# A two-layer hybrid decoder trunk on one Trainium2 core: the weight loads of the gated FFN's groups in the order in which their buffers come free, and the residual turned later

## The chip, the cores and the metric

The kernel runs on 1 core of one Trainium2 chip, in one launch. The metric is device time in microseconds (us), the median of several executions. Engines are named as in the profile: PE (TensorE), DVE (VectorE), ACT (ScalarE), POOL (GpSimd), SP (SyncE, which here only issues DMAs). SPq is SP's queue of DMA issues.

## The reference, cut to what matters

`x` is 512 tokens by 1024 channels, f32. There are two layers; each adds a mixer and then a gated FFN, and the change touches only the FFNs and the product that ends the second one.

```python
for l in range(2):
    h = rms_norm(x, mix_norm_w[l])
    y = even_mixer(h, ...) if l % 2 == 0 else odd_mixer(h, ...)
    x = x + y @ w_out[l]
    h = rms_norm(x, ffn_norm_w[l])                    # 512 x 1024
    x = x + (silu(h @ w_gate[l]) * (h @ w_up[l])) @ w_down[l]   # 1024 -> 2816 -> 1024
return rms_norm(x, final_norm_w)
```

## The kernel before

**Split products.** Every f32 product is made from operands that are split into a high and a low part (`hi` on ACT, `lo` on DVE) and multiplied as high*high + high*low + low*high. Weights come in tiles of 128x1024 f32 (512 KB). A tile's two parts live in one of the RING = 4 slots of `wring`; ACT may write a slot only when PE has used the tile four before it.

**The gated FFN.** `h @ w_gate` and `h @ w_up` share their left operand, and the kernel computes most of both (GROUPED = 5 groups of 512 columns each; 256 columns are done plainly before them) by a scheme with 7 block products for 8. A group `j` of layer `l` has GLU_PRODUCTS = 7 products of two tiles (p0, p1), so 14 steps: G_M11 (steps 0, 1), G_M12 (2, 3), G_M22 (4, 5), G_M21 (6, 7), G_SUM (8, 9), G_LAST (10, 11), G_ALL (12, 13). Their weights come from four buffers of two tiles each:

- `x_part` holds G_M11's tiles, then is added to in place three times for G_M21, G_SUM and G_ALL;
- `raw` holds G_M12's tiles; `y_part` holds G_M22's and is then added to `x_part` by DVE (`sum_weights`, after steps 6 and 8);
- `w_part` is loaded and grown once for G_LAST.

SP issues the plain loads (`load_group`, `load_part`). POOL issues the growing ones: a DMA with `accum_op=add` that adds a part of the weights to a buffer in SBUF (`grow_group`, L907): two on `x_part` for G_M21 after G_M11's `lo`, two on `w_part`, and two on `x_part` for G_ALL after G_SUM's `lo`. A next group's buffer may be loaded when the last `lo` that reads it is done: `raw` after G_M12, `y_part` after the sums of steps 6 and 8, `w_part` after G_LAST, `x_part` after G_ALL, the last two steps.

PE begins a group's G_M11 when DVE has taken G_LAST's result of the group before out of its PSUM bank (`gate_first`, L1600), which stands on DVE behind the `lo` of G_M11's p1 (step 1). It begins G_M12 after `up_second` (L1603), behind the `lo` of G_M12's p1 (step 3), and G_M21 after `q` (L1589, step 7).

**The residual.** The last product makes its result by tokens, while x is kept by channels, so x is turned: DVE transposes 32x32 blocks of xT into `turned` (`turn_residual`, L1630, eight instructions), and 16 DMAs on SP's queue (`residual_blocks`, L817, 128 KB each in pieces of 32 floats) put the blocks in their places in `resid`. `turned` lies over chunks of AF that ACT writes from group 2 on, and ACT waits for all 16 there (`keep_turned`, at step 7 of group 2 in layer 1).

**Order of the work.** All five engines run instruction lists written out by hand with semaphores; each engine and each DMA queue takes its list in order, so a DMA whose wait isn't over holds all that stand behind it.

**The last product** (`w_down` of layer 1) follows the same scheme on 42 tiles: `left_high` on ACT and `left_low` on DVE split its left operand's pieces (`place_even`, `place_odd`), and `halves` on DVE makes the sums that later products need.

A growth of one weight sum in DRAM (`w_sums`, 12 DMAs of POOL in the first mixer) is the same before and after.

Of the kernel before, what the change touches and what calls it, by code (L numbers as in the profile page):

```python
# [23 lines left out]
KD = D // P  # L24
# [12 lines left out]
GROUPED = 5  # L37
# [33 lines left out]
P_12, P_11, P_21, P_22, P_SUM, P_LAST, P_ALL = range(PRODUCTS)  # L71
# [9 lines left out]
def piece_rows(i):  # L81

    return range(2 * i, min(2 * i + 2, HALF))
# [18 lines left out]
def glu_tile(l, j, a, p):  # L102

    return T_GLU[l] + j * GLU_STEPS + 2 * a + p
# [7 lines left out]
def weights_summed(l, j, p):  # L112

    return l * SUMS + LEFT_SUMS + 2 * j + p + 1


def part_count(l, j):

    return 16 * (1 + GROUPED * l + j + 1)
# [22 lines left out]
def last_tile(g):  # L142

    return T_DN1 + g
# [222 lines left out]
def build(nc, sums_d, x_d, w_d, glu_d, last_d, vec_d, row_d, const_d, rope_d, final_d, out_d):  # L367
# [9 lines left out]
    def at(name, shape, dt, offset):  # L377
        t = nc.alloc_sbuf_tensor_at(name, [P] + list(shape), dt, offset=offset)
        return t, offset + (int(np.prod(shape)) * size[dt] + 31) // 32 * 32

    base = 16512
    xT, p = at("xT", [KD, S], f32, base)
    raw, p = at("raw", [RAW, TILE], f32, p)
    wring, p = at("wring", [RING, 2, TILE], f32r, p)
    at_H = p
    HH, p = at("HH", [KD, 2, S], f32r, p)
    consts, p = at("consts", [6 + len(LEVELS), P], f32, p)
    at_work = p
    hbuf, p = at("hbuf", [2, S], f32, p)
    sqb, p = at("sqb", [2, S], f32, p)  # L390
    squares, _ = at("squares", [4, S], f32, at_work)
    ssq, p = at("ssq", [S], f32, p)
    rstd, p = at("rstd", [S], f32, p)
    vec, p = at("vec", [N_VEC], f32, p)
# [117 lines left out]
    x_part, q = at("x_part", [2, TILE], f32, q)  # L512
# [5 lines left out]
    turned, _ = at("turned", [NB, KD, P], f32, at_A + 6 * S * 4)  # L518
# [14 lines left out]
    resid, _ = at("resid", [NB, 2, S], f32, base)  # L533
# [57 lines left out]
    def kept_chunk(k):  # L591

        return AF[:, k] if k < ENDING else kept_end[:, k - ENDING]
# [32 lines left out]
    def sem(name):  # L626
        if name not in sems:
            sems[name] = nc.alloc_semaphore(name)
        return sems[name]

    def slot_round(t):

        return t // RING + 1
# [9 lines left out]
    def raw_before(t):  # L643

        return max(u for u in range(t) if (uses_raw(u) or u < FIRST) and u % RAW == t % RAW and (t >= FIRST + RAW or u == t - FIRST))
# [13 lines left out]
    feed_hi, feed_sq, ssq_done, h_ready = map(sem, ("feed_hi", "feed_sq", "ssq_done", "h_ready"))  # L659
# [43 lines left out]
    FINAL = 4  # L703
# [16 lines left out]
    def _(sp):  # L720
# [41 lines left out]
        def load_part(l, place, sem_at, j, kh, u):  # L762

            for p in range(2):
                n = sem_at + p
                if j:
                    t = glu_tile(l, j - 1, G_LAST if place is w_part else G_M22 if place is y_part else G_ALL, p)
                    sp.wait_ge(lo_ready[t % RING], slot_round(t))
                    if place is y_part:
                        sp.wait_ge(sem("lhs_made"), weights_summed(l, j - 1, p))  # L770
                sp.wait_ge(part_loaded[n], part_count(l, j) - 16)
                sp.dma_start(place[:, p], glu_d[l, j, kh, u][:, p * TILE:(p + 1) * TILE]).then_inc(part_loaded[n], 16)

        def load_group(l, j):

            if j == 0:
                load_part(l, x_part, 0, j, 0, 0)
            for p in range(2):
                t = glu_tile(l, j, G_M12, p)
                before = raw_before(t)  # L780
                sp.wait_ge(hi_ready[before % RING], slot_round(before))
                sp.wait_ge(lo_ready[before % RING], slot_round(before))
                sp.dma_start(raw[:, t % RAW], glu_d[l, j, 0, 1][:, p * TILE:(p + 1) * TILE]).then_inc(raw_loaded[t % RAW], 16)
            load_part(l, y_part, 2, j, 1, 1)
            load_part(l, w_part, 4, j, 1, 0)
            if j + 1 < GROUPED:
                load_part(l, x_part, 0, j + 1, 0, 0)

        sp.wait_ge(tile_used, T_OUT0 + RING)
        for j in range(GROUPED):  # L790
            load_group(0, j)
# [12 lines left out]
                src = w_d[bass.ds(r * RING + (j - AWAY), 1)].rearrange("a p c -> (a p) c")  # L804
                sp.dma_start(raw[:, j % RAW], src).then_inc(raw_loaded[j % RAW], 16)

        def residual_blocks(m):

            a, b = m // 4, m % 4
            if m == 0:  # L810
                sp.wait_ge(sem("resid_turned"), KD)
                sp.wait_ge(feed_sq, KD * FINAL)
                sp.wait_ge(h_ready, KD * FINAL)
                sp.wait_ge(sem("lhs_scaled"), 2 * KD)
            to = resid[32 * b:32 * b + 32].rearrange("p t u (n x c) -> p (t u n) x c", x=4, c=32)
            from_ = turned[32 * a:32 * a + 32].rearrange("p t n (x c) -> p (t n) x c", c=32)
            sp.dma_start(to[:, :, a], from_[:, :, b]).then_inc(sem("resid_loaded"), 16)  # L817

        for t in range(loop_end * RING, T_GLU[1]):
            sp.wait_ge(hi_ready[(t - RAW) % RING], slot_round(t - RAW))  # L820
            sp.wait_ge(lo_ready[(t - RAW) % RING], slot_round(t - RAW))
# [1 line left out]
        sp.wait_ge(tile_used, T_GU1)  # L823
        for j in range(GROUPED):
            load_group(1, j)
            if j == 0:
                for m in range(16):
                    residual_blocks(m)

        for i in range(PIECES):  # L830
            t = last_tile(i)
# [3 lines left out]
            n = len(piece_rows(i)) * S  # L835
# [12 lines left out]
        for i in range(PIECES):  # L848
            t = last_tile(P_21 * PIECES + i)
# [7 lines left out]
        n = OUT_ORDER[-1]  # L857
# [622 lines left out]
    def _(dve):  # L1480
# [132 lines left out]
        def halves(r):  # L1613

            if r == 0:
                dve.wait_ge(sem("ffn_mul"), MULS + 2)
            else:
                dve.wait_ge(sem("glu_kept"), 4 * GROUPED + (2 * r if r < HALF - 2 else 4 * GROUPED - HALF + 1 + r))
            first, second = kept_chunk(2 * r), kept_chunk(2 * r + 1)
            V.tensor_tensor(first[:, 2 * P:S], first[:, 2 * P:S], second[:, 2 * P:S], ALU.subtract).then_inc(sem("halves_made"), 1)  # L1620
            dve.wait_ge(sem("halves_made"), 2 * r + 1)
            V.tensor_tensor(pfull[:, r], first[:, 0:2 * P], first[:, 2 * P:S], ALU.subtract).then_inc(sem("halves_made"), 1)
# [9 lines left out]
        def after_glu_lo(l, g):  # L1632

            j, step = divmod(g, GLU_STEPS)
            if j:
                if step == 1:
                    glu_results(l, j - 1, "gate_first")
                elif step == 3:
                    glu_results(l, j - 1, "up_second")
                    glu_results(l, j - 1, "first")  # L1640
                elif step == 4:
                    glu_results(l, j - 1, "second")
            elif l and 4 <= step < 8:
                for n in (2 * step - 8, 2 * step - 7):
                    turn_residual(n)
            if step == 6:
                sum_weights(l, j, 0)
            elif step == 7:
                glu_results(l, j, "q")
            elif step == 8:  # L1650
                sum_weights(l, j, 1)
            elif step == 9:
                glu_results(l, j, "up_first")
            elif step == 11:
                glu_results(l, j, "gate_second")
            if l and step in (10, 12):
                if j:
                    halves(2 * j - 1 + (step - 10) // 2)
                elif step == 10:
                    halves(0)  # L1660
# [6 lines left out]
        def left_low(a, i):  # L1667

            dve.wait_ge(sem("ffn_hi"), split_count(a, i))
            high = place(a, i, 0).bitcast(f32)  # L1670
            if a in (P_21, P_22):
                ins = V.scalar_tensor_tensor(place(a, i, 1), full_left(a, i), -1.0, high, ALU.mult, ALU.subtract)
            else:
                ins = V.tensor_tensor(place(a, i, 1), full_left(a, i), high, ALU.subtract)  # L1674
            ins.then_inc(sem("ffn_lo"), 1)
# [94 lines left out]
        def last_product():  # L1770

            dve.wait_ge(sem("resid_loaded"), 16 * 16)
            for g in range(PRODUCTS * PIECES):
                last_lo(g)
                a, i = divmod(g, PIECES)
                if g < RING:
                    group_end(1, g)
                if g == 4:
                    halves(9)
                    halves(10)  # L1780
                    left_low(P_12, 4)
                    left_low(P_12, 5)
                if a == P_22:
                    cross(P_LAST, i)
                if g < 36:
                    left_low(a + 1, i)
                if a == P_SUM:
                    cross(P_ALL, i)
                if i == 4 and a >= 2:
                    after_product(a - 1)  # L1790
# [34 lines left out]
        for n in range(KD):  # L1825
            dve.wait_ge(x_loaded[X_PART[n]], 16)
            feed_lo(0, n)
            if n < 2 * HALVED:
                t, half = n // 2, slice(n % 2 * S, (n % 2 + 1) * S)
# [53 lines left out]
        for kind, a in even_order():  # L1883
# [26 lines left out]
            elif kind == "gate_evac":  # L1910
                c, m = SLOTS[a][1:]
# [18 lines left out]
            elif kind == "tap":  # L1930
                c, k = a
# [1072 lines left out]
```

## Time and profile before

| | before |
|---|---|
| median of 3 runs | 1222.06 us (1219.14 to 1222.58) |
| profiled execution, its own time | 1221.2 us |
| its span, first to last instruction | 1219.4 us |
| PE matmul busy | 1186.4 us, 97% of the span |
| DVE, ACT, POOL busy | 837.8, 619.4, 141.9 us |
| mean granted clock of PE | 0.990 |
| chain that ended last, PE's share | 85%; SPq 2%, nearly all on L817 |

Matmul ends are modelled, so a busy PE is not PE at its peak; but PE's idle time is what waits for other engines cost here. A time such as 926 us is counted from the span's start. The first FFN's groups run from about 245 to 446 us, the second's from 886 to 1105 us, the last product from there to 1203 us.

### The profile page before, as it was taken

How to read it: one execution, taken by the hardware profiler on the slowest of the kernel's cores; microseconds unless marked ns; L12 is line 12 of the kernel's file. 1: busy time of each engine (PE TensorE's matmuls, PEld its weight loads, DVE VectorE, ACT ScalarE, POOL GpSimd, SP SyncE). 2: the span in 40 equal slices, each digit the busy share in tenths (PEclk: the TensorE clock that was granted, in tenths of full speed). 3: DMA queues.
4: the chain of work that ended last, by engine and by line, in shares of the span. 5: the costliest groups of instructions: out<-in, count | busy, mean ns of one | idle time of the engine just before them, and what ended most of it. 6: DMA issues, size and time to landing. Idle time of an engine off the chain costs nothing.

```text
span 1219.4 us, 15948 instructions
## 1 busy us (share of the span) xinstructions
PE 1186.4 (97%) x5791; PEld 959.2 (79%) x5791; DVE 837.8 (69%) x1273; ACT 619.4 (51%) x992; POOL 141.9 (12%) x251
## 2 busy tenths in 40 slices
PE   9999999999999999999999999999995899999998
PEld 7876648888888888888888788888874788887886
DVE  6787886786667763336777666546791777788796
ACT  6354455655555543235584254444551555556564
POOL 0010000011111100000003814300010111110120
PEclk9999999999999999999999999999998899999999
DMA  6388621567877843222322211012558587777981
GB/s 246 121 230 184 153 54 52 192 102 209 206 155 159 247 97 104 95 96 74 110 78 68 87 36 53 27 60 70 181 96 187 124 210 204 171 175 271 226 151 69
DMA packets 63694, 165.45 MB, mean 136 GB/s; under 512 B 22658, under 2 KB 22914, under 8 KB 63362
## 3 DMA queue, kind: packets, MB, share of 16 engines
q1 hardware_dynamic: 49746, 114.33, 28.9%
q0 software_dynamic: 12960, 48.76, 22.4%
q10 hardware_dynamic: 912, 1.35, 0.4%
q8 instruction: 47, 0.77, 0.3%
q14 instruction: 29, 0.24, 0.1%
HBM read 155.87 MB, written 10.75 MB: 137 GB/s over the span
## 4 chain that ended last, share of the span: by engine, by line
PE 85%; DVE 6%; ACT 3%; SPq 2%; issue 2%; DMA 2%; ACTq 0%; DVEq 0%
PE PS L2263 82%; SPq L817 2%; PE PS L2559 1%; DMA first_raw<-w_stream 1%; DVE wring L1571 1%; PE PS L2339 1%; DVE cacc L1939 0%; DMA x_part<-w_glu 0%; ACTq L1275 0%; DVE wring L1794 0%; DMA raw<-w_glu 0%; ACT wring L1036 0%; ACT wring L984 0%; DVE turned L1630 0%; DVE amax L1857 0%
## 5 line engine op out<-in xcount | busy, mean ns | idle before, releaser
L2263 PE MATMUL PS<-HH,wring 128*128 128x512 f32 x1176 | 288.7, 397 | 0.9 <-DVE vd L2191 0.9
L2263 PE MATMUL PS<-wring,HH 128*128 128x512 f32 x1152 | 268.7, 392 | 17.6 <-DVE glu_s L1603 17.3
L2263 PEld LDWEIGHTS PS<-wring,HH 128*128 128x128 f32 x1152 | 217.2, 189 | 63.4 <-DVE glu_s L1603 17.7
L2263 PEld LDWEIGHTS PS<-HH,wring 128*128 128x128 f32 x1176 | 215.0, 188 | 44.0 <-issue 1.3
L1571 DVE TENSOR_TENSOR wring<-x_part,wring 128x1024 fp32r<-128x1024 f32 x80 | 97.9, 1224 | 77.3 <-ACT wring L1036 77.2
L1794 DVE TENSOR_TENSOR wring<-raw,wring 128x1024 fp32r<-128x1024 f32 x91 | 111.9, 1232 | 46.2 <-ACT wring L984 46.2
L984 ACT ACTIVATE wring<-raw 128x1024 fp32r<-128x1024 f32 x91 | 95.7, 1056 | 94.4 <-PE PS L2263 68.8
L1036 ACT ACTIVATE wring<-x_part 128x1024 fp32r<-128x1024 f32 x80 | 84.6, 1060 | 107.1 <-PE PS L2263 45.9
L2263 PE MATMUL PS<-AS,wring 128*128 128x512 f32 x528 | 120.4, 389 | 0.0
L2263 PE MATMUL PS<-wring,left_minus 128*128 128x512 f32 x480 | 113.8, 393 | 1.6 <-DVE glu_q L1589 1.6
L2263 PEld LDWEIGHTS PS<-AS,wring 128*128 128x128 f32 x528 | 99.0, 188 | 20.5
L2263 PEld LDWEIGHTS PS<-wring,left_minus 128*128 128x128 f32 x480 | 88.9, 188 | 19.9 <-DVE glu_q L1589 2.0
L907 POOL DMA_DIRECT2D x_part<-w_glu x40 | 34.6, 865 | 454.4 <-DVE wring L1571 454.4
L2263 PE MATMUL PS<-AA,wring 128*128 128x512 f32 x264 | 63.4, 394 | 0.4 <-DVE AA L1873 0.3
L2263 PE MATMUL PS<-wring,place_even 128*128 128x512 f32 x264 | 61.1, 390 | 1.2 <-DVE place_even L1674 1.2
L2263 PEld LDWEIGHTS PS<-wring,place_even 128*128 128x128 f32 x264 | 49.4, 188 | 11.8 <-issue 1.6
L2263 PEld LDWEIGHTS PS<-AA,wring 128*128 128x128 f32 x264 | 49.1, 188 | 11.6 <-issue 1.0
L2263 PE MATMUL PS<-wring,left_diff 128*128 128x512 f32 x240 | 56.5, 391 | 0.4 <-DVE hbuf L1600 0.4
L2263 PEld LDWEIGHTS PS<-wring,left_diff 128*128 128x128 f32 x240 | 44.8, 188 | 10.7 <-DVE hbuf L1600 1.5
L1665 DVE TENSOR_TENSOR AS<-AF,AS 128x512 fp32r<-128x512 f32 x20 | 13.8, 689 | 48.0 <-ACT AS L1087 48.0
L2263 PE MATMUL PS<-wring,place_odd 128*128 128x512 f32 x198 | 45.4, 389 | 0.0
L2263 PEld LDWEIGHTS PS<-wring,place_odd 128*128 128x128 f32 x198 | 37.2, 188 | 7.7
(367 smaller groups left out, 1687.8 us busy)
## 6 DMA issues: line engine op xcount, KB each, us to landing
raw<-w_stream SPq DMA_DIRECT2D x91, 512.0 KB, 3.5
x_part<-w_glu POOLq DMA_DIRECT2D x40, 512.0 KB, 6.3
x_part<-w_glu SPq DMA_DIRECT2D x20, 512.0 KB, 4.3
raw<-w_glu SPq DMA_DIRECT2D x20, 512.0 KB, 5.8
y_part<-w_glu SPq DMA_DIRECT2D x20, 512.0 KB, 8.6
w_part<-w_glu SPq DMA_DIRECT2D x20, 512.0 KB, 13.9
w_part<-w_glu POOLq DMA_DIRECT2D x20, 512.0 KB, 7.1
w_sums<-w_last POOLq DMA_DIRECT2D x12, 704.0 KB, 6.7
```

What stands on the lines that cost most here:

```text
L817: sp.dma_start(to[:, :, a], from_[:, :, b]).then_inc(sem("resid_loaded"), 16)
L907: nc.gpsimd.dma_start(to, addend[:, p * TILE:(p + 1) * TILE], accum_op=ALU.add).then_inc(added[d % ADDING], 16)
L984: nc.scalar.activation(wring[:, t % RING, 0], raw_tile(t), ACT.Copy).then_inc(hi_ready[t % RING], 1)
L1036: nc.scalar.activation(wring[:, t % RING, 0], glu_source(t, a, p), ACT.Copy).then_inc(hi_ready[t % RING], 1)
L1571: V.tensor_tensor(wring[:, t % RING, 1], glu_source(t, a, p), wring[:, t % RING, 0].bitcast(f32), ALU.subtract).then_inc(lo_ready[t % RING ...
L1665: V.tensor_tensor(AS[:, k % RING, 1], kept_chunk(k), AS[:, k % RING, 0].bitcast(f32), ALU.subtract).then_inc(sem("ffn_lo"), 1)
L1794: V.tensor_tensor(wring[:, t % RING, 1], raw_tile(t), wring[:, t % RING, 0].bitcast(f32), ALU.subtract).then_inc(lo_ready[t % RING], 1)
L2263: return nc.tensor.matmul(out, lhsT, rhs, start=start, stop=stop, skip_group_check=adds)
L2339: last = nc.tensor.transpose(PS[:, bank, blk(j)], src[:, u % 2, blk(j)], ident)
L2559: last = nc.tensor.transpose(PS[:, banks[c], blk(b)], glu_result(b)[:, blk(c)], ident)
```

## The change

Three edits, all of them in the order of instructions; no operation is added or removed.

1. **Loads.** In both layers SP's list for group `j` was: raw(j), y(j), w(j), x(j+1). It becomes raw(j), y(j), w(j), x(j), so that of a next group's eight loads `x_part`'s two, whose buffer comes free last, stand last and not first.
2. **Residual.** The 16 DMAs stood behind x(1) and ahead of raw(1). Now 8 stand between raw(2) and y(2), and 8 between y(2) and w(2). DVE's eight transposes move from steps 4 to 7 of group 0 to steps 10, 12 and 13.
3. **Last product.** At its tile 4 DVE splits pieces 4 and 5 of the first left operand before it makes `halves(9)` and `halves(10)`, no longer after.

```diff
@@ SP
-            if j == 0:
-                load_part(l, x_part, 0, j, 0, 0)
+        def load_group(l, j):
+
+            if j == 0:
+                load_part(l, x_part, 0, j, 0, 0)
+            load_raw(l, j)
+            if l and j == 2:
+                for m in range(8):
+                    residual_blocks(m)
             load_part(l, y_part, 2, j, 1, 1)
+            if l and j == 2:
+                for m in range(8, 16):
+                    residual_blocks(m)
             load_part(l, w_part, 4, j, 1, 0)
-            if j + 1 < GROUPED:
-                load_part(l, x_part, 0, j + 1, 0, 0)
+            if j:
+                load_part(l, x_part, 0, j, 0, 0)
...
             load_group(1, j)
-            if j == 0:
-                for m in range(16):
-                    residual_blocks(m)
@@ DVE, after_glu_lo
-            elif l and 4 <= step < 8:
-                for n in (2 * step - 8, 2 * step - 7):
+            elif l and step in (10, 12, 13):
+                for n in {10: (0, 1), 12: (2, 3, 4), 13: (5, 6, 7)}[step]:
                     turn_residual(n)
@@ DVE, last_product
                 if g == 4:
+                    left_low(P_12, 4)
+                    left_low(P_12, 5)
                     halves(9)
                     halves(10)
-                    left_low(P_12, 4)
-                    left_low(P_12, 5)
```

(`load_raw` holds the two loads of `raw` as they stood in `load_group`, now L793.)

SP's list in layer 1, from the end of group 0's loads to x(2), before the change:

```order
L772 DMA w_part<-w_glu 128x1024 [waits x_loaded5]
L772 DMA x_part<-w_glu 128x1024 [waits x_loaded0,lo_ready1]
L772 DMA x_part<-w_glu 128x1024 [waits x_loaded1,lo_ready2]
L817 DMA resid<-turned 32x32x32 [waits h_ready,lhs_scaled,feed_sq,resid_turned]
L817 DMA resid<-turned 32x32x32 x15
L783 DMA raw<-w_glu 128x1024 [waits lo_ready3,hi_ready3]
L783 DMA raw<-w_glu 128x1024 [waits lo_ready0,hi_ready0]
L772 DMA y_part<-w_glu 128x1024 [waits x_loaded2,lhs_made,lo_ready1]
L772 DMA y_part<-w_glu 128x1024 [waits x_loaded3,lhs_made,lo_ready2]
L772 DMA w_part<-w_glu 128x1024 [waits x_loaded4,lo_ready3]
L772 DMA w_part<-w_glu 128x1024 [waits x_loaded5,lo_ready0]
```

and group 2's loads in the list of the changed kernel, which SP issues while group 1 runs:

```order
L793 DMA raw<-w_glu 128x1024 [waits lo_ready1,hi_ready1]
L793 DMA raw<-w_glu 128x1024 [waits lo_ready2,hi_ready2]
L784 DMA resid<-turned 32x32x32 [waits h_ready,lhs_scaled,feed_sq,resid_turned]
L784 DMA resid<-turned 32x32x32 x7
L772 DMA y_part<-w_glu 128x1024 [waits x_loaded2,lhs_made,lo_ready3]
L772 DMA y_part<-w_glu 128x1024 [waits x_loaded3,lhs_made,lo_ready0]
L784 DMA resid<-turned 32x32x32 x8
L772 DMA w_part<-w_glu 128x1024 [waits x_loaded4,lo_ready1]
L772 DMA w_part<-w_glu 128x1024 [waits x_loaded5,lo_ready2]
L772 DMA x_part<-w_glu 128x1024 [waits x_loaded0,lo_ready3]
L772 DMA x_part<-w_glu 128x1024 [waits x_loaded1,lo_ready0]
```

Each load now stands behind loads whose waits end earlier than its own, and the 16 small DMAs stand ahead of y(2), w(2) and x(2).

DVE's list in group 0 of layer 1, before (from step 4 to the first growth's `q`):

```order
L1630 STREAM_TRANSPOSE turned<-xT 128x4x128 x2
L1571 TENSOR_TENSOR wring<-y_part,wring 128x1024
L1630 STREAM_TRANSPOSE turned<-xT 128x4x128 x2
L1571 TENSOR_TENSOR wring<-x_part,wring 128x1024
L1630 STREAM_TRANSPOSE turned<-xT 128x4x128 x2
L1578 TENSOR_TENSOR x_part<-x_part,y_part 128x1024
L1571 TENSOR_TENSOR wring<-x_part,wring 128x1024
L1630 STREAM_TRANSPOSE turned<-xT 128x4x128 x2
L1589 TENSOR_TENSOR glu_q<-PS,glu_q 128x512 x2
```

and in the changed kernel, from step 10 on:

```order
L1637 STREAM_TRANSPOSE turned<-xT 128x4x128 x2
L1627 TENSOR_TENSOR AF<-AF 128x256
L1629 TENSOR_TENSOR pfull<-AF 128x256
L1578 TENSOR_TENSOR wring<-w_part,wring 128x1024
L1602 TENSOR_TENSOR glu_q<-glu_q,PS 128x512 x2
L1578 TENSOR_TENSOR wring<-x_part,wring 128x1024
L1637 STREAM_TRANSPOSE turned<-xT 128x4x128 x3
L1578 TENSOR_TENSOR wring<-x_part,wring 128x1024
L1637 STREAM_TRANSPOSE turned<-xT 128x4x128 x3
L1578 TENSOR_TENSOR wring<-x_part,wring 128x1024 x2
L1607 TENSOR_TENSOR hbuf<-PS,glu_s 128x512 x2
```

The transposes have left the stretch ahead of `q` (L1589) and stand round the two `lo` of G_ALL.

## Rows read from the trace of the kernel before

**Rows 1.** Waits of PE, longest first (four of fifteen)

```profile
PE PS L2263 <- DVE glu_s L1603: 17.3, 1, 17.3
PE PS L2263 <- DVE glu_q L1589: 1.6, 1, 1.6
...
PE PS L2263 <- DVE place_even L1674: 1.2, 1, 1.2
...
PE PS L2263 <- DVE hbuf L1600: 0.4, 1, 0.4
```

**Rows 2.** Timeline of SP: start, duration, what (xcount)

```profile
918.16 20.49 SPq L817 DMA_DIRECT2D resid<-turned  x16
938.74 1.11 SPq L783 DMA_DIRECT2D raw<-w_glu  x2
```

**Rows 3.** Chain that ended last, 914 to 965 us: start, us, what

```profile
919.81 2.43 SPq L817
...
932.82 0.67 SPq L817
...
949.18 7.77 PE PS L2263 x24
...
957.82 5.49 PE PS L2263 x24
```

**Rows 4.** One stretch of 1 us: busy time by engine, clock, DMA share, GB/s

```profile
936.00:937.00 1.00, 0.00 (x0) 0.00 (x0) 0.00 (x0) 0.00 (x0) 0.00 (x0) 0.75 1.09 180
```

**Rows 5.** Timeline of DVE, group 0 of layer 1 (one of four pairs)

```profile
893.40 1.30 DVE L1630 STREAM_TRANSPOSE turned<-xT 128x512 f32<-128x512 f32 x2
```

**Rows 6.** Timeline of DVE, last product, tile 4

```profile
1117.14 0.43 DVE L1620 TENSOR_TENSOR AF<-AF 128x256 f32<-128x256 f32 x1 [2.85 <-ACT AF L1043]
...
1118.73 0.68 DVE L1674 TENSOR_TENSOR place_even<-AF,place_even 128x512 fp32r<-128x512 f32 x1
```

**Rows 7.** Chain that ended last, from group 1 to 2 of layer 0

```profile
317.05 5.21 DMA x_part<-w_glu
```

**Rows 8.** Timeline of PE: first matmuls of groups 2 and 3, layer 1

```profile
985.80 1.52 PE L2263 MATMUL PS<-wring,left_diff 128*128 128x512 f32 x6
...
1025.70 5.60 PE L2263 MATMUL PS<-wring,left_diff 128*128 128x512 f32 x24
```

**Rows 9.** Timeline of ACT there: `hi` of G_ALL p1, of the next G_M11 p1

```profile
1015.08 1.06 ACT L1036 ACTIVATE wring<-x_part 128x1024 fp32r<-128x1024 f32 x1 [0.43 <-PE PS L2263]
...
1021.32 1.06 ACT L1036 ACTIVATE wring<-x_part 128x1024 fp32r<-128x1024 f32 x1 [1.69 <-DMA x_part<-w_glu]
```

**Rows 10.** Timeline of DVE there: `lo` of G_LAST p0, G_ALL p1, then `gate_first`, `sum_weights` p1

```profile
1008.01 1.23 DVE L1571 TENSOR_TENSOR wring<-w_part,wring 128x1024 fp32r<-128x1024 f32 x1 [0.42 <-ACT wring L1036]
...
1016.17 1.22 DVE L1571 TENSOR_TENSOR wring<-x_part,wring 128x1024 fp32r<-128x1024 f32 x1 [0.69 <-ACT wring L1036]
...
1023.56 1.28 DVE L1600 TENSOR_TENSOR hbuf<-PS,glu_s 128x512 f32<-128x512 f32 x2
...
1042.72 1.22 DVE L1578 TENSOR_TENSOR x_part<-x_part,y_part 128x1024 f32<-128x1024 f32 x1
```

**Rows 11.** Timeline of POOL there: the growth of G_ALL p1

```profile
1006.69 0.87 POOL L907 DMA_DIRECT2D x_part<-w_glu  x1 [2.62 <-DVE wring L1571]
```

**Rows 12.** DMA issues of 1017:1017.7, 938:941: xcount, KB, us to landing

```profile
x_part<-w_glu SPq DMA_DIRECT2D x1, 512.0 KB, 3.9
...
y_part<-w_glu SPq DMA_DIRECT2D x2, 512.0 KB, 6.4
```

**Rows 13.** DMA issues of POOL at 1006.69, 984.80, 925.12 and 1136.83

```profile
x_part<-w_glu POOLq DMA_DIRECT2D x1, 512.0 KB, 6.2
...
x_part<-w_glu POOLq DMA_DIRECT2D x1, 512.0 KB, 12.1
...
x_part<-w_glu POOLq DMA_DIRECT2D x1, 512.0 KB, 7.8
...
kept<-w_last POOLq DMA_DIRECT2D x1, 256.0 KB, 9.1
```

More of the change, by code:

```diff
@@ L772, in load_part, with residual_blocks, load_raw @@
                 sp.dma_start(place[:, p], glu_d[l, j, kh, u][:, p * TILE:(p + 1) * TILE]).then_inc(part_loaded[n], 16)
-        def load_group(l, j):
-            if j == 0:
-                load_part(l, x_part, 0, j, 0, 0)
+        def residual_blocks(m):
+            a, b = m // 4, m % 4
+            if m == 0:
+                sp.wait_ge(sem("resid_turned"), KD)
+                sp.wait_ge(feed_sq, KD * FINAL)
+                sp.wait_ge(h_ready, KD * FINAL)
+                sp.wait_ge(sem("lhs_scaled"), 2 * KD)
+            to = resid[32 * b:32 * b + 32].rearrange("p t u (n x c) -> p (t u n) x c", x=4, c=32)
+            from_ = turned[32 * a:32 * a + 32].rearrange("p t n (x c) -> p (t n) x c", c=32)
+            sp.dma_start(to[:, :, a], from_[:, :, b]).then_inc(sem("resid_loaded"), 16)
+        def load_raw(l, j):
             for p in range(2):
@@ L805, in _ @@
                 sp.dma_start(raw[:, j % RAW], src).then_inc(raw_loaded[j % RAW], 16)
[L807 to L817, printed above, removed]
         for t in range(loop_end * RING, T_GLU[1]):
```

## The prediction

> **What bounds the kernel now.** I read the table of busy times first: PE's matmuls fill nearly all of the span, so a gain can only come from PE's idle time and from stretches at the low clock. So the second view is the list of PE's waits [rows 1]. One wait is 17.3 us long, and three more lie where the edits are: 1.6, 1.2 and 0.4 us; all others lie elsewhere.
>
> The timeline of SP tells what the long one is. After x(1) SP issues the residual's 16 small DMAs, which takes from 918.16 to 938.65, and only then raw(1) [rows 2]. PE is through G_M11(1) at 949.18 - 17.3 = 931.9 [rows 1, 3] and can't start G_M12(1): `up_second` stands on DVE behind the `lo` of raw(1), and PE goes on at 949.18 [rows 3]. SP is the bound in this stretch, and it is held by its queue. The issues are slow only for a part of the time: two by 919.81, then six up to 932.82, 2.2 us each, then eight in 5.8 us, 0.73 each [rows 2, 3]. The slow part ends when POOL's growth of 925.12 has landed, 7.8 us later at 932.9 [rows 13]. So small DMAs give way to a growth, and hardly slow it: alone it takes 6.2.
>
> The pause also costs clock. PE went idle at 931.9 and the granted clock fell within 936 to 937 to half [rows 4]; the first 24 matmuls after it took 7.77 us, against 5.49 for the next 24 [rows 3]: 2.3 us more.
>
> **What the groups look like where nothing stalls.** Let t be the time since PE began a group's G_M11. From group 2 to 3 of layer 1 the period is 39.9 us [rows 8]. The `hi` of G_ALL p1 begins at t = 29.3, held by PE [rows 9]; its `lo` ends at 31.6 [rows 10], x's p1 is issued, lands after 3.9 [rows 12] at 35.5, where ACT waited for it [rows 9]; `gate_first` ends at 39.0 [rows 10]. That is 3.5 us from landing to release, and PE needs it at 39.9: the margin is 0.9 us. The growth of x's p1 for G_ALL is issued at t = 20.9 [rows 11] and lands at 27.1; it may land at 29.3 without being noticed, and at 30.1 before PE waits. Every group boundary hangs on this chain.
>
> **The change, part by part.**
>
> *The long wait.* Raw(1)'s two loads now stand behind w(0) and x(0) and wait for G_M12(0) alone, with nothing of the residual ahead of them, so they land some 20 us before they are wanted. The 17.3 us go, and with them the 2.3 us of half clock: 19.6. What hides the loads is group 0 itself.
>
> *The transposes.* Four pairs of 1.30 us [rows 5] stood on DVE ahead of `q`, 5.2 us, and PE waited 1.6 for `q` [rows 1]. Without them `q` is in time: gain 1.6. At steps 12 and 13 three each take 1.95 us. Ahead of the `lo` of G_ALL p1 DVE has 0.7 us of idle time in a quiet group [rows 10]; 1.95 - 0.7 = 1.3 us late, less the margin of 0.9, is 0.4 in the worst order I can make. Bounds 0 and 1.3 (no margin); I take 0.3.
>
> *The last product.* Four instructions of `halves` fill DVE from 1117.14 to 1118.73, where the split of piece 4 begins [rows 6], for which PE waits 1.2 us [rows 1]. The new order gives these 1.6 us to the split first; the wait goes: gain 1.2. The halves are then late by about 1 us, the two splits; they feed products whose tiles aren't next.
>
> *Layer 0.* The 0.4 us wait [rows 1] stands where x's p1 took 5.21 us to land [rows 7], with raw, y and w issued right behind it. With nothing behind it I take 3.9: gain 0.4.
>
> Sum of the gains: 17.3 + 2.3 + 1.6 + 1.2 + 0.4 = 22.8 us.
>
> *The residual's new place.* The 16 DMAs still go through SP's queue, now in group 1. The first eight follow raw(2), at t of about 3; they delay only y(2), which isn't wanted for 40 us. The second eight follow y(2)'s p1, which waits for the second weight sum, done at t = 1043.94 - 1025.70 = 18.2 [rows 8, 10]. Behind them stand w(2), free at t = 23.4 [rows 10], and x(2), whose p1 is free at 31.6 and is on the chain above. Price: from 18.7 two quick issues to 20.3; then at 2.2 us each until the growth of t = 20.9 has landed, 7.8 later at 28.7: four; two more at 0.73: t = 30.2. Then w p0, w p1, x p0, x p1 in one burst. In the burst of 938.74 [rows 2] the third and fourth load took 6.4 us from issue [rows 12], the fourth being issued some 1.6 after the first: it lands 8.0 after the burst's start. So x p1 lands at 38.2, release at 41.7, a wait of 1.8 us. Bounds: nothing, if all eight go at 0.73 (t = 24.6, ahead of x); and 5.0, if they take the 14.7 us of the first eight before (t = 33.4), and 7.3 with the clock's 2.3, since the pause would then be about as long as the one after which the clock fell. The first eight meet w's growths, which now come early, and may make y's p1 late too; so I take 3.0, above the middle estimate.
>
> *Loads beside growths, in every group.* Before, a next group's raw, y and w were issued behind x, in a burst, when no growth was near its due time. Now y's p1 (t = 18.2), w's p0 (23.4) and p1 (about 26) travel while POOL grows x for G_ALL. How much this delays the growth that may land until 30.1 no row shows directly. From below: small DMAs beside it, 7.8 us [rows 13], lands at 28.7, no wait. From above: 12.1 us, beside six loads and another growth [rows 13]: lands at 33.0, a wait of 2.9 per boundary. The nearest row is a growth beside loads in the last product, 9.1 us [rows 13], though of half the size: 30.0, just in time. Seven boundaries (four per layer less the one above) at 0.3 us: 2.0.
>
> The sum of the losses is 0.3 + 3.0 + 2.0 = 5.3; the gain left is 17.5. Against the profiled execution's own time, 1221.2, this makes 1203.7. The median of the runs is 0.9 above that execution, so I predict 1204.5 us.
>
> The Trainium skill speaks against this part (*DMA: Bandwidth & Descriptors*, section *Queues, rings and completion order*): each DMA engine goes round robin between the queues that have work, a packet at a time. By it POOL's growths and SP's loads would halve the engines between them, whoever is urgent. The 12.1 us agree with that; the 7.8 us beside the small DMAs don't look like halves by time.
>
> **The rivals.**
>
> *Growths late everywhere.* If a growth shares evenly with each load that overlaps it, it pays for them: a load in a burst adds (8.0 - 3.9) / 3 = 1.4 us, so three moved loads add up to 4.2: the growth lands at up to 31.3, a wait of 1.2 at seven boundaries, 8.4; and the residual's place then costs its upper 5.0. Net gain 22.8 - 8.4 - 5.0 - 0.3 = 9.1: 1213. For it: the 12.1 us. Against: these loads come one by one, and the first of them is over before the critical growth begins to move data. By the Trainium skill's rule above this is the case that would come.
>
> *All hidden.* The eight go at 0.73 and no growth is late: 22.8 gained, 1199.3. For it: small DMAs hardly disturb growths, and 128 KB at 0.73 us is quick. Against: the slow issues before were slow just because two growths ran, and two run here.
>
> *Slower or no gain.* One mechanism at every boundary: the growth of G_ALL p1 lands not at 27 but past 33. From 12.1 us on, eight boundaries lose 2.9 each, 23.2, which is all that is gained; with the residual's 3.0 the kernel stands at 1225.5. It decides from a landing time of about 12.5 us. Against: it needs three loads spread over 8 us to do what six in a burst did.
>
> *The wait only moves.* SP's 20.5 us could reappear whole at group 1 to 2. They can't: the list is cut by y(2), which waits until 18.2, and raw(2) is ahead; what can move is the 5.0 to 7.3 above, 1207 to 1209, held in the range of the likeliest.
>
> **How the numbers follow.** The likeliest case, a chance of 0.55, has its own range from 1200.5 (the residual's place at 1, no growth late) to 1209 (7.3 there, or growths 0.9 late at each boundary). All hidden 0.15; growths late everywhere 0.24, 1210 to 1217; slower or no gain 0.06. Leaving out the tail below 1199 and what lies above 1215, less than 2 in 10, gives 1199 to 1215. A measurement of this kernel can tell about 0.3%, 3.7 us, from no change: 1218.4 and 1225.7 are the limits. The first three cases lie below the first: faster 0.94. The last is split: same 0.03, slower 0.03.
>
> **What the changed profile would show.** Right: PE's wait for `glu_s` gone and no stretch of half clock near 940; no wait for `glu_q` or `place_even`; SP's 16 small DMAs in two runs of eight, the second ending near t = 30 of group 1; one wait of 1 to 5 us for `hbuf` (`gate_first`) at the start of G_M11(2) in layer 1. Wrong: waits of 1 us and more for `hbuf` at most starts of groups, with POOL's growths of G_ALL taking 10 us and more to land; or the clock at half again in group 2; or, the other way, no wait there at all.

## The result, and the profile after

The changed kernel takes 1205.28 us, the median of 4 runs (1204.76 to 1206.66); the kernel before, beside it, 1221.98. The ratio is 0.987, with a 95% interval of 0.9852 to 0.9887. The profiled execution took 1204.76 us with a span of 1203.0, 16.4 less than before's 1219.4. The forecast was 1204.5.

The waits of PE after the change, the three longest of ten (engine, who released it: us in all, times, longest):

```profile
PE PS L2270 <- DVE hbuf L1607: 6.5, 2, 6.2
PE PS L2270 <- POOL rstd L872: 1.3, 1, 1.3
PE PS L2270 <- DVE vd L2198: 0.9, 1, 0.9
```

Against [rows 1]: the waits for `glu_s` (17.3), `glu_q` (1.6) and `place_even` (1.2) are gone, and so is layer 0's 0.4. One new wait of 6.2 us has come, for `hbuf` (`gate_first`). All lines are 7 further down than before: L1600 is now L1607.

The timeline of SP after, from the loads of group 1 to those of group 3 (start, duration, what), against [rows 2]:

```profile
911.27 3.24 SPq L772 DMA_DIRECT2D x_part<-w_glu  x2
923.47 2.18 SPq L793 DMA_DIRECT2D raw<-w_glu  x2
925.83 14.51 SPq L784 DMA_DIRECT2D resid<-turned  x8
940.44 3.03 SPq L772 DMA_DIRECT2D y_part<-w_glu  x2
943.53 12.71 SPq L784 DMA_DIRECT2D resid<-turned  x8
956.33 1.10 SPq L772 DMA_DIRECT2D w_part<-w_glu  x2
957.53 0.86 SPq L772 DMA_DIRECT2D x_part<-w_glu  x2
969.91 2.17 SPq L793 DMA_DIRECT2D raw<-w_glu  x2
```

Group 1 begins at 922.32. The second eight end at 956.24, t = 33.9, and x(2) goes out behind them and behind w(2). What that does is in the timelines of ACT and PE (the brackets hold the idle time ahead and what ended it):

```profile
953.30 1.06 ACT L1043 ACTIVATE wring<-x_part 128x1024 fp32r<-128x1024 f32 x1 [1.97 <-DMA x_part<-w_glu]
964.00 2.25 ACT L1043 ACTIVATE wring<-x_part 128x1024 fp32r<-128x1024 f32 x2 [8.66 <-DMA x_part<-w_glu]
```

```profile
922.32 5.78 PE L2270 MATMUL PS<-wring,left_diff 128*128 128x512 f32 x24 [0.28 <-DVE hbuf L1607]
968.76 7.62 PE L2270 MATMUL PS<-wring,left_diff 128*128 128x512 f32 x24 [6.21 <-DVE hbuf L1607]
976.22 5.61 PE L2270 MATMUL PS<-wring,HH 128*128 128x512 f32 x24
```

The first row of ACT is the `hi` of G_ALL p1: it waited 1.97 us for POOL's growth, which landed 9.9 us after its issue at 943.37 (the quiet group's took 6.2 [rows 13]). The second is the `hi` of the next G_M11, both tiles at once, at 964.00. PE stood still from 962.55 to 968.76, and its first 24 matmuls took 7.62 us against 5.61 for the next. So the new place of the residual cost 6.2 us of waiting and 2.0 of half clock.

The windows of 1 us there (PE busy, granted clock, DMA share, GB/s) show when the clock fell, as [rows 4] did:

```profile
964.00:965.00 1.00, 0.00 (x0) 1.00 0.22 86
965.00:966.00 1.00, 0.00 (x0) 0.99 0.00 0
966.00:967.00 1.00, 0.00 (x0) 0.50 0.02 8
```

PE had been idle for 3.4 us when the clock went from 2.4 to 1.2 GHz; it came back between 972 and 973, some 4 us after PE had begun again.

### The profile page after: what moved, and what is told of

The parts are those of the page before. It is cut to its first block, busy times and chain, and to the rows that moved or that the text cites. A ratio compares the mean times of both kernels' runs of the same rounds, so it can differ in the third digit from the quotient of the medians.

```text
span 1203.0 us, 15948 instructions
## 1 busy us (share of the span) xinstructions
PE 1184.6 (98%) x5791; PEld 958.4 (80%) x5791; DVE 837.4 (70%) x1273; ACT 619.1 (51%) x992; POOL 142.0 (12%) x251
## 4 chain that ended last, share of the span: by engine, by line
PE 88%; DVE 5%; ACT 3%; issue 2%; SPq 1%; DMA 1%; ACTq 0%; POOL 0%; DVEq 0%; POOLq 0%
PE PS L2270 85%; PE PS L2566 1%; SPq L784 1%; DMA x_part<-w_glu 1%; DVE wring L1578 1%; ACT wring L1043 1%; PE PS L2346 1%; DVE cacc L1946 0%; ACTq L1282 0%; PE PS L2650 0%; DVE wring L1801 0%; ACT wring L991 0%; DVE turned L1637 0%; DVE out L2261 0%; DVE hbuf L1607 0%
## 6 DMA issues: line engine op xcount, KB each, us to landing
w_part<-w_glu POOLq DMA_DIRECT2D x20, 512.0 KB, 11.2
```

## Experiments

Each was timed beside the kernel before in the same session (its medians there: 1219.8, 1220.6 and 1219.9 us), so runs are compared by their ratios.

### The second eight behind x(2)

```diff
-            if l and j == 2:
-                for m in range(8, 16):
-                    residual_blocks(m)
             load_part(l, w_part, 4, j, 1, 0)
             if j:
                 load_part(l, x_part, 0, j, 0, 0)
+            if l and j == 2:
+                for m in range(8, 16):
+                    residual_blocks(m)
```

> Two theories of the 6.2 us wait for `gate_first` at the start of G_M11(2) in layer 1 and the half clock behind it (2.0 us). *Order in SP's queue:* w(2) and x(2) were issued late because the second eight small DMAs stood ahead of them (12.7 us, to 956.2), and the growth for G_ALL(1) was late (9.9 us) because the eight ran beside it. With the eight behind x(2) they begin at about t = 32, beside the growths of group 2 as the first eight ran beside those of group 1 (about 14 us), and are through some 3 us before ACT waits for the residual at step 7 of group 2. Both 6.2 and 2.0 go: 1205.3 - 8.2 = 1197.1 us, a wait for `hbuf` there of at most 0.5 us, the clock full. *Growths beside the loads of y(2) and w(2):* the growth lands late (9 us and more) with or without the small DMAs; the wait shrinks to 2 to 4 us at the same place and the time is 1200 to 1203 us.

Measured: 1198.06 us, ratio 0.9824 (0.9809 to 0.984); the span is 1195.6, 7.4 less than the changed kernel's. Its timeline of SP, and the first matmuls of group 2:

```profile
946.28 3.05 SPq L772 DMA_DIRECT2D w_part<-w_glu  x2
951.73 3.04 SPq L772 DMA_DIRECT2D x_part<-w_glu  x2
954.82 19.78 SPq L784 DMA_DIRECT2D resid<-turned  x8
```

```profile
963.17 5.73 PE L2270 MATMUL PS<-wring,left_diff 128*128 128x512 f32 x24 [0.29 <-DVE hbuf L1607]
```

w(2) and x(2) go out at their buffers' own times, the wait is 0.3 us and the clock stays full: the order in SP's queue was the cause. The growth for G_ALL p1 still took 8.3 us beside y(2)'s loads, and that costs nothing. With the second eight beside it too it took 9.9 us in the changed kernel's first profile and 8.9 in its second. So against the 6.2 of a quiet group most of the delay goes with y(2)'s loads, and less of it with the second eight. The eight themselves took 19.8 us, more than the 14 expected: ACT waited 2.83 us for them at step 7 of group 2, PE not at all. This version beats both kernels. Once more, in another session:

> The version with the second eight behind x(2) once more, beside its neighbours: 0.982 of the kernel before, 1197 to 1199 us, no wait above 0.5 us for `hbuf`.

1197.74 us, ratio 0.9823 (0.981 to 0.9836), waits for `hbuf` 0.43 and 0.16 us, the growth for G_ALL p1 8.8 us.

### Four and four

```diff
-                for m in range(8, 16):
+                for m in range(8, 12):
                     residual_blocks(m)
             load_part(l, w_part, 4, j, 1, 0)
             if j:
                 load_part(l, x_part, 0, j, 0, 0)
+            if l and j == 2:
+                for m in range(12, 16):
+                    residual_blocks(m)
```

> Of the second eight small DMAs four stay behind y(2), four go behind x(2): the dose between the changed kernel and the one with all eight moved. *Order in SP's queue:* in the changed kernel the fourth of the eight is issued at 952.6, just as the growth lands, so the growth is about as late as there (9 to 10 us); but x(2) p1 is then held by the `lo` of G_ALL p1 alone (t = 33 instead of 34.2 and a burst of four loads): the wait for `hbuf` is 1.5 to 3 us and the clock stays full, 1198.5 to 1200 us. If only the count of DMAs ahead of x(2) mattered, in proportion: half of 6.2, 3.1 us, and 1201 us. *Growths beside the loads:* no different from the run with all eight moved.

Measured: 1201.42 us, ratio 0.9854 (0.9836 to 0.9871). SP and PE:

```profile
941.49 11.20 SPq L784 DMA_DIRECT2D resid<-turned  x4
952.79 1.11 SPq L772 DMA_DIRECT2D w_part<-w_glu  x2
953.99 1.15 SPq L772 DMA_DIRECT2D x_part<-w_glu  x2
```

```profile
966.24 5.74 PE L2273 MATMUL PS<-wring,left_diff 128*128 128x512 f32 x24 [3.38 <-DVE hbuf L1610]
```

Four DMAs hold SP for 11.2 us where eight held it for 12.7: most of the price of small DMAs in this place is one stretch of time, not a count, and each DMA issued behind it adds 0.7 us. The wait was 3.4 us, above the 1.5 to 3 that I gave, since SP came free only at 952.7 and w and x then went out in one burst. Wait and time lie nearer to what the count alone would give (3.1 us, 1201 us), so this run's time doesn't decide between the two; SP's rows do. The clock stayed full.

### All sixteen behind x(2)

```diff
-            if l and j == 2:
-                for m in range(8):
-                    residual_blocks(m)
             load_part(l, y_part, 2, j, 1, 1)
-            if l and j == 2:
-                for m in range(8, 16):
-                    residual_blocks(m)
             load_part(l, w_part, 4, j, 1, 0)
             if j:
                 load_part(l, x_part, 0, j, 0, 0)
+            if l and j == 2:
+                for m in range(16):
+                    residual_blocks(m)
```

> All sixteen of the residual's small DMAs behind x(2), none beside the growth for G_ALL(1). This also shows how long that growth takes beside the loads of y(2) and w(2) alone. *Order in SP's queue:* x(2) in time, no wait for `hbuf`, growth within 7.5 us; the sixteen take about 20 us from t = 32 and end some 3 us after ACT wants them at step 7 of group 2, and raw(3) goes out some 8 us later than before, still early: a wait of 0 to 2 us in group 2, 1197 to 1199 us. *Growths beside the loads:* the growth takes 9 us and more, and a wait of 1 to 3 us for `hbuf` stays: 1199 to 1202 us.

Measured: 1203.67 us, ratio 0.9872 (0.9856 to 0.9887), 5 us worse than expected. Rows of SP, ACT and PE:

```profile
954.36 26.77 SPq L784 DMA_DIRECT2D resid<-turned  x16
```

```profile
983.08 1.08 ACT L1047 ACTIVATE AF<-PS 128x512 f32<-128x512 f32 x2 [7.54 <-DMA resid<-turned]
```

```profile
963.20 5.74 PE L2267 MATMUL PS<-wring,left_diff 128*128 128x512 f32 x24 [0.90 <-DVE hbuf L1604]
983.82 0.41 PE L2563 MATMUL PS<-consts,hbuf 128*128 128x128 f32 x2 [3.08 <-ACT AF L1047]
984.64 7.32 PE L2267 MATMUL PS<-wring,left_minus 128*128 128x512 f32 x24
```

The sixteen took 26.8 us, not 20, and ended 7.5 us after ACT wanted them; PE waited 3.1, and the clock fell with it (7.32 against 5.7 for 24 matmuls). So the residual can also be too late: eight behind x(2) fit, sixteen don't. The growth for G_ALL p1, beside the loads of y(2) and w(2) alone and each at its own time, took 6.8 us, within the 7.5 expected, and the wait for `hbuf` was 0.9: the loads by themselves don't make it late.

### The growths for G_ALL(1) shrunk

```diff
-                nc.gpsimd.dma_start(to, addend[:, p * TILE:(p + 1) * TILE], accum_op=ALU.add)...
+                few = 16 if (l, j) == (1, 1) and n >= 4 else TILE
+                nc.gpsimd.dma_start(to[:, 0:few], addend[:, p * TILE:p * TILE + few], accum_op=ALU.add)...
```

> The changed kernel with POOL's two growths for G_ALL(1) in layer 1 cut to 16 of their 1024 columns (so most of the last weight sum of group 1 is left out); all waits and the order of SP's queue stay. *The growth makes the small DMAs slow:* the second eight go at about 0.73 us each, SP is through with them near 949.5 instead of 956.2, w(2) and x(2) p0 are issued at once, x(2) p1 as soon as its `lo` ends (t = 31.6); no wait for `hbuf`, full clock: 8.2 us less than the changed kernel, 1197 us. *They are slow by themselves, or beside y(2)'s two loads:* SP is through with them at 953 to 956 and 3 to 6 us of the wait stay: 1199 to 1205 us.

Measured: 1197.41 us, ratio 0.9818 (0.98 to 0.9836). SP, then PE:

```profile
941.07 9.77 SPq L784 DMA_DIRECT2D resid<-turned  x8
950.94 1.11 SPq L772 DMA_DIRECT2D w_part<-w_glu  x2
952.14 1.92 SPq L772 DMA_DIRECT2D x_part<-w_glu  x2
```

```profile
963.20 5.76 PE L2271 MATMUL PS<-wring,left_diff 128*128 128x512 f32 x24 [1.03 <-DVE hbuf L1608]
```

Neither theory came out whole. Without the growths' data the time is about that of the version with the second eight behind x(2), and the wait 1.0 us, but the eight still take 9.8 us and not the 5.8 of eight at 0.73: y(2)'s two loads, ahead of them in the same queue, hold them too. The trace bears this out: the third small DMA's issue stood from 943.05 to 947.17, y(2)'s second load landed at 947.4, and from 943 to 945 us the shrunk growths took 3.2% of the engines' time. No run had neither the loads nor the growths there.

### All sixteen ahead of y(2)

```diff
-                for m in range(8):
+                for m in range(16):
                     residual_blocks(m)
             load_part(l, y_part, 2, j, 1, 1)
-            if l and j == 2:
-                for m in range(8, 16):
-                    residual_blocks(m)
```

> All sixteen of the residual's DMAs between raw(2) and y(2): the second eight run beside the same growths for G_ALL(1) as in the changed kernel, but without y(2)'s two 512 KB loads ahead of them in SP's queue. With the growths shrunk and y(2)'s loads there they took 9.8 us; with both 12.4 to 14.3. *Both hold them, and add up:* 5.8 us when nothing does, 4.0 for y(2)'s loads, 2.6 to 4.5 for the growths; so here 8.4 to 10.3 us, through near t = 28. y(2), w(2) and x(2) p0 then go in one burst and x(2) p1 lands about 1.5 us late: 1198 to 1200 us. *The growths alone are enough:* 12 us and more, to t = 31, a wait of 4 us and more for `hbuf`: 1202 to 1205 us. *The loads in the queue alone:* 5.8 us, no wait, 1197 us.

Measured: 1203.45 us, ratio 0.9865 (0.9851 to 0.9879). SP and ACT:

```profile
926.66 26.94 SPq L784 DMA_DIRECT2D resid<-turned  x16
953.71 1.10 SPq L772 DMA_DIRECT2D y_part<-w_glu  x2
...
955.85 1.19 SPq L772 DMA_DIRECT2D x_part<-w_glu  x2
```

```profile
963.33 1.06 ACT L1040 ACTIVATE wring<-x_part 128x1024 fp32r<-128x1024 f32 x1 [8.72 <-DMA x_part<-w_glu]
```

The last eight took from 940.6 to 953.6, 13 us, though no load stood ahead of them: the growths alone are enough, and the two causes don't add. PE waited 4.8 us for `hbuf` and lost clock again; y(2), w(2) and x(2) all went out late, and a wait of 0.8 us came at the start of the next group too.

Why they are slow is in the DMA queues (packets, MB, time of the packets as a share of 16 engines; q0 is POOL's, q1 SP's), here 943 to 945 us of this run, in which SP's queue holds nothing but small DMAs:

```profile
q0 software_dynamic: 76, 0.31, 86.0%
q1 hardware_dynamic: 128, 0.02, 10.5%
```

and 954 to 957 us of the changed kernel, after the growth:

```profile
q1 hardware_dynamic: 4298, 0.54, 108.7%
```

A small DMA is some 1,024 packets of 128 bytes. Alone 4298 pass in 3 us, 0.71 us for a DMA, which is the 0.7 us of an issue. Beside a growth in full flow 128 pass in 2 us, fewer than two for each of its 76 large packets of about 4 KB; at that rate one DMA would take 16 us. It never comes to that, because the growths have thinner stretches: from 942 to 952 us, with both growths in it, 4949 small packets pass, 2.1 us for a DMA. The Trainium skill (*DMA: Bandwidth & Descriptors*, section *Queues, rings and completion order*) has each DMA engine go round robin between the queues that have work, a packet at a time. The rows agree in kind: turns are shared, time isn't, and the queue with the large packets gets 86% of it against 10.5%. The small ones are starved, and SP stands at its next issues meanwhile: three of the last eight took 2.0, 4.3 and 2.8 us.

### The loads' order alone, and the old order with the residual away

The loads alone: the changed kernel with the residual's 16 DMAs behind the loads of group 0, the transposes at steps 4 to 7 and the `halves` first.

```diff
             load_group(1, j)
+            if j == 0:
+                for m in range(16):
+                    residual_blocks(m)
```

> The new order of the loads alone: the residual's 16 DMAs stand behind the loads of group 0 and ahead of all of group 1's, the transposes are at steps 4 to 7, the `halves` ahead of the splits, all as in the kernel before. The residual can then start as soon as it is turned (t about 18), no longer behind x(1) at t = 32. *Order in SP's queue:* 16 DMAs take some 20.5 us, to t = 39; raw(1) lands in time, but x(1) p1 lands about 8 us later, at t = 47 instead of 35.5, so PE waits some 9 us for `hbuf` at the start of G_M11(1), plus 2 of half clock; with 1.6 for `q` and 1.2 for the last product back and no wait at G_M11(2): 1205.3 + 11.3 - 8.2 + 2.8 = 1211 us. So most of the 17.3 us wait goes by the load order alone and part of it moves. *Rival:* the residual's DMAs are quick there (0.73 each, 12 us in all, to t = 30): no wait at G_M11(1), 1200 us.

Measured: 1215.82 us, ratio 0.9966 (0.9953 to 0.9979). SP and ACT:

```profile
902.71 19.84 SPq L784 DMA_DIRECT2D resid<-turned  x16
```

```profile
934.89 1.06 ACT L1040 ACTIVATE wring<-x_part 128x1024 fp32r<-128x1024 f32 x1 [16.54 <-DMA x_part<-w_glu]
```

The sixteen took the 20 us I gave them, but x(1) stood last in a burst of eight loads and landed only at 934.9 and later: the wait for `hbuf` was 13.7 us, not 9. So the new order of loads alone turns the 17.3 us wait into one of 13.7; it pays only with the residual moved too.

The other half: the kernel before's order of loads, with the residual in group 2 behind w(2) and the two other edits as changed.

```diff
             load_part(l, w_part, 4, j, 1, 0)
+            if l and j == 2:
+                for m in range(16):
+                    residual_blocks(m)
             if j + 1 < GROUPED:
                 load_part(l, x_part, 0, j + 1, 0, 0)
```

> The kernel before with its own order of loads (x of the next group ahead of that group's raw, y and w), but the residual's sixteen DMAs in group 2 behind w(2), and the transposes and the `halves` as in the changed kernel. Asks what the load order is worth once the residual is out of the way. The long wait at G_M12(1) goes. The sixteen start near 957.5, behind x(2), raw(2), y(2) and w(2), and take 27 us as in the run with all of them behind x(2): ACT waits about 10 us for them at step 7 of group 2, of which PE sees 5 to 6, plus 2 us of half clock: 1203 to 1205 us. If the load order itself were worth something beside that (by the prediction 0.4 in layer 0), waits of 0.4 us and more would also come back at other starts of groups.

Measured: 1212.27 us, ratio 0.9931 (0.9917 to 0.9946), 8 us above what I expected. Of SP and PE:

```profile
959.71 30.48 SPq L784 DMA_DIRECT2D resid<-turned  x16
```

```profile
992.84 0.66 PE L2559 MATMUL PS<-consts,hbuf 128*128 128x128 f32 x2 [11.46 <-ACT AF L1043]
```

The sixteen, behind a burst of loads and beside four growths, took 30.5 us; ACT waited 15.0 and PE 11.5. In the old order x(2) is ahead of raw, y and w, so all of them go out late and the residual later still. It also shows in layer 0: this run has a wait of 1.2 us there at the start of a group, before has 0.4, and no profile in the new order has one. What the new order is worth beyond that this run doesn't settle, since it tries one place of the residual in the old order. Its own trace shows another: behind w(1) SP has nothing to issue from 921.1 to 952.98 us, when x(2)'s buffer comes free, 32 us in a row, and sixteen small DMAs in a row took 20 to 30 us wherever they stood. The old order with the residual there was not run; it is a rival to moving the loads at all.

### The transposes back, and the halves back

The changed kernel with each small edit undone, and the changed kernel itself as their comparison.

> The changed kernel unaltered, beside the next three, as what they are compared with. 1204 to 1206 us, with 6.2 us for `hbuf` at G_M11(2) and half clock behind it as in its first profile. The stretch near 783 us, which no edit touches, ran at half clock for some 4 us in the profile of before and of the loads alone and at full clock in the others: if it is chance of the run, single runs of one kernel lie about 1.6 us apart for it.

1204.70 us, ratio 0.9871 (0.9853 to 0.9889).

```diff
-            elif l and step in (10, 12, 13):
-                for n in {10: (0, 1), 12: (2, 3, 4), 13: (5, 6, 7)}[step]:
+            elif l and 4 <= step < 8:
+                for n in (2 * step - 8, 2 * step - 7):
```

> The changed kernel with the eight transposes back at steps 4 to 7 of group 0, all else as changed. If they cost what the prediction says: PE's wait of 1.6 us for `q` comes back, the wait of 0.3 us at the start of G_M11(1) goes: 1.3 us more than the changed kernel. *Rival:* the 1.6 us are swallowed by the margin behind (0.9 at most), or the 0.3 us is due to the growth beside the loads and stays: between 0.7 and 1.6 us more.

1206.63 us, ratio 0.9887 (0.9869 to 0.9906). The interval doesn't part it from the changed kernel, but its waits do:

```profile
PE PS L2270 <- DVE hbuf L1607: 5.9, 1, 5.9
PE PS L2270 <- DVE glu_q L1596: 1.6, 1, 1.6
```

The 1.6 us for `q` is back, and the wait at the start of G_M11(1) is gone: `hbuf` is waited for once. With the transposes at steps 12 and 13 that wait was 0.28 and 0.75 us in the changed kernel's two profiles, and 0 to 0.61 in the others that have them there. So the move gives 1.6 and takes back at most 0.75. From the start of group 0 to that of group 1 it is 40.0 us with the transposes back, and 38.5 and 39.0 in the changed kernel's two profiles: a net 1.0 to 1.5. That the transposes cause the wait at G_M11(1) isn't shown, since two of the profiles that have them there have no wait.

```diff
+                    halves(9)
+                    halves(10)
                     left_low(P_12, 4)
                     left_low(P_12, 5)
-                    halves(9)
-                    halves(10)
```

> The changed kernel with the `halves` ahead of the splits again in the last product. PE's wait of 1.2 us for `place_even` comes back and the time is 1.2 us longer; if another engine was as late there, PE's wait would be shorter and the time within 0.5 us of the changed kernel.

1205.30 us, ratio 0.9875 (0.9857 to 0.9893), which by itself tells nothing of 1.2 us. The waits do:

```profile
PE PS L2270 <- DVE hbuf L1607: 6.1, 2, 5.7
...
PE PS L2270 <- DVE place_even L1681: 1.2, 1, 1.2
```

and the span, 1204.2, is 1.5 longer than the 1202.7 of the changed kernel's second profile, whose waits for `hbuf` add up to 6.2.

## Why the prediction was right, and where it was wrong

The likeliest case came, inside its own range, with its sign, place and mechanism. But one of the signs that the prediction lists as *wrong* came too: the clock was at half again at the start of group 2, behind a wait of 6.2 us where 1 to 5 were given. The 16.4 us of span come apart by the starts of the groups as follows.

| from the start of | before, us | after, us | gained, us |
|---|---|---|---|
| the kernel to group 0 of layer 1 | 885.95 | 883.80 | 2.15: layer 0 0.5, the stretch at 783 us 1.6 |
| group 0 to group 1 | 40.13 | 38.52 | 1.6 |
| group 1 to group 2 | 59.72 | 46.44 | 13.3 |
| group 2 to group 3 | 39.90 | 41.92 | -2.0: half clock |
| group 3 to the last product | 79.80 | 79.88 | -0.1 |
| the last product to the end | 113.9 | 112.4 | 1.5 |

*The long wait*: 19.6, as predicted. From the start of group 1 to that of group 2 in layer 1 it was 59.72 us before and is 46.44, of which 6.21 are the new wait; 59.72 - 19.6 = 40.1 and 46.44 - 6.21 = 40.2 are the same period. *The transposes*: the 1.6 for `q`, as predicted, and the undoing shows it. The 0.3 lost at the start of group 1 is there in this profile, but it is 0 to 0.75 in the others, so the 0.3 predicted is neither shown nor refuted; the net of group 0 is 1.6. *The last product*: the 1.2 of waiting went and came back with the edit; the part is 1.5 shorter, and 0.3 of that no wait explains. *Layer 0*: 0.5 instead of 0.4, by the start of its group 3 (405.79 before, 405.26 after).

*Loads beside growths*: I charged 2.0 us, 0.3 at each of seven boundaries. The periods of the quiet groups are 39.9 to 40.1 us after as before, so it cost 0.3 us at most. The growth for G_ALL p1 is indeed later, 6.4 us for group 2's against 6.2 [rows 13] and 8.3 beside y(2)'s loads without small DMAs behind them, but it lands when PE's own pace releases its `hi`. The rival *growths late everywhere* fell with that: the one growth that is late enough to be waited for is the one with y(2)'s loads in full and the second eight beside it.

*The residual's new place*: this step failed in its size. I took 3.0 us, with 7.3 as the upper bound; it cost 8.2, 6.2 of waiting and 2.0 of clock. The eight ended at t = 33.9, not 30.2, and x(2) p1 landed in time for 964.0, t = 41.7, not 38.2. The chain that ended last has the two slow issues:

```profile
944.17 5.45 SPq L784
...
949.66 2.91 SPq L784
```

I had the slow stretch end at t = 28.7, since I let the growth land after 7.8 us; it took 9.9 (8.9 in the second profile), and the stretch ended at 30.3: 1.5 us. And I priced the slow issues at 2.2 us each, an average of [rows 3], so that only two would be left at the end of the stretch; with only these two issued in it, five were left at 0.7: 2.2 us more. A third number I put at nothing: y(2)'s two loads, which are ahead of the eight in SP's queue. From 944 to 949 us of the changed kernel, most of the first slow issue, the two queues moved

```profile
q1 hardware_dynamic: 257, 0.95, 63.4%
q0 software_dynamic: 105, 0.36, 37.5%
```

and only 42 of all these packets were small: SP's queue was moving y(2)'s loads, and the growth had 37.5% of the engines' time beside them. With all sixteen ahead of y(2), so without these loads, the growth took 8.1 us. By themselves, in the run with the growths shrunk, the loads make 9.8 us out of 5.8. When the slow stretch starts varies: in this profile the issue of y(2)'s second load stood for 2.3 us and the eight began at t = 21.2, not 18.7; in the changed kernel's second profile they began at 18.8 and took 14.3. The end is t = 33.9 and 33.1. The burst's 8.0 us from first issue to last landing was right: 956.33 to 964.0 is 7.7. The clock's 2.3 I had put behind the upper bound alone; a pause of 6.2 us brought 2.0.

The forecast lies 0.8 us from the median although this term is 5.2 too small, and that is luck. In the profiles the span fell by 16.4 where 17.5 were forecast: loads beside growths gave back 1.7, 1.6 came from a stretch that no edit touches (below), and the small edits and layer 0 gave 0.7 more than I had put.

*All hidden* (1199.3) was the wrong case for this kernel, but it is about what the residual's better place gives: 1198 with the second eight behind x(2).

## What to carry to other kernels

Where a queue is worked off in order, give each DMA a place by the time at which its buffer comes free and by its own deadline; then look at what it passes. Moving the loads without the residual, or the residual without the loads, gave 0.3 and 0.7% (the latter with the two small edits), both moved, with the second eight behind x(2), 1.8%; each half was tried in one place only. Small DMAs have no fixed price: read the packets of both queues in the very stretch in which they will run, for beside a transfer of large packets, in another queue or ahead in their own, they stood here until about the time when it had landed, and everything behind them in their queue waited too. When a wait of several us moves, ask again whether what is left of it still costs clock.

## What the runs showed of the hardware

How long PE may pause without loss of clock isn't one number in these runs. After 3.4 us of waiting (four and four) the clock stayed at its full level and the 24 matmuls took 5.74 us; after 3.1 us (all sixteen behind x(2)) it fell to half and they took 7.32. The two pauses differ in what stands round them. In the second PE came back at 983.82 with eight matmuls of 128 columns, and the 24 large ones began only at 984.64, 3.9 us after it had stopped; and it had stood for 0.9 us some 20 us earlier. The first has neither: its large matmuls begin right after the pause. Which of these counts, if either, no run tells. The windows of 1 us of the second, with the clock falling late in the second of them:

```profile
983.00:984.00 1.00, 0.18 (x2) 1.00 0.97 172
984.00:985.00 1.00, 1.00 (x9) 0.84 0.88 328
985.00:986.00 1.00, 1.00 (x3) 0.50 1.02 418
```

The other surprise is at 783 us, in the odd mixer, which is the same in all these kernels. In the profile of before the clock is at half there for some 4 us:

```profile
783.00:784.00 1.00, 1.00 (x7) 0.50 0.00 0
```

It is so in the run of the loads alone too, and at full clock in all the others. It costs 1.6 us of the profile's span when it comes, in kernels that are alike up to that point, so it is a matter of the single run, and one profile against another can't tell less than that without a look there.
